# Placing the weight slots and the activation area at multiples of 1024 bytes in an fp32r transformer kernel

## What is computed

```python
x = x + 0.5 * swiglu(rmsnorm(x, ffn1_norm[l]), w_ffn1_in[l], w_ffn1_out[l])
u = rmsnorm(x, mix_norm[l])
c_q, c_kv, k_r, hq, hf, hi, hgate, mq, gate_logits = split_sizes(u @ w_in[l], IN_SPLITS)
y_mla = mla_branch(...) @ w_o_mla[l]        # causal attention from latents
y_hg = hgrn2_branch(...) @ w_o_hg[l]        # gated recurrence in chunks of 64
y_mem = memory_branch(...) @ w_o_mem[l]     # attention over 256 memory tokens
merged = gates[:, :, 0] * y_mla + gates[:, :, 1] * y_hg + gates[:, :, 2] * y_mem
x = x + merged @ w_out[l]
x = x + 0.5 * swiglu(rmsnorm(x, ffn2_norm[l]), w_ffn2_in[l], w_ffn2_out[l])
```

## The kernel before

| | address | mod 1024 | mod 64 |
|---|---|---|---|
| `x` (8192 bytes) | 16512 | 128 | 0 |
| `vecs`, gains and other small vectors (928 bytes) | 24704 | 128 | 0 |
| `c1`, constants | 25632 | 32 | 32 |
| `x_ssq`, `x_diag`, `x_sq` | 28736, 29760, 30784 | 64 | 0 |
| `raw0` to `raw2` | from 31904, every 8192 | 160 | 32 |
| `whi0` to `whi3` | from 56480, every 4096 | 160 | 32 |
| `wlo0` to `wlo3` | from 72864, every 4096 | 160 | 32 |
| `arena` | 90080 | 992 | 32 |

## Time and profile before

### The profile page before, as it was taken

How to read it: one execution, slowest core, us unless ns; L and a number is a source line. 1 busy time by engine, 2 the same in 40 slices (tenths; PEclk the granted TensorE clock), 3 DMA queues, 4 the chain that set the end, 5 groups by cost and what they waited for, 6 DMA issues and landing times.

```text
span 2501.2 us, 49272 instructions
## 1 busy us (share of the span) xinstructions
PE 2475.3 (99%) x20948; PEld 2416.1 (97%) x20948; DVE 1673.0 (67%) x2315; ACT 1279.4 (51%) x1812; POOL 406.9 (16%) x357
## 2 busy tenths in 40 slices
PE   9999999999999999999999999999999999999998
PEld 8999999999999999999999999999999999999998
DVE  7765776866667567877666666846666665846664
ACT  5544656554445455565444545535444444634543
POOL 4012120300200210102012014402011013512001
PEclk9999999999999999999999999999999999999999
DMA  6555433555555543345555554303555555402553
GB/s 238 186 186 186 159 128 122 191 192 189 179 190 188 179 176 139 120 164 186 186 186 211 191 197 167 117 18 134 187 186 185 186 186 182 152 2 86 196 185 126
DMA packets 57675, 410.11 MB, mean 164 GB/s; under 512 B 6384, under 2 KB 6640, under 8 KB 8688
## 3 DMA queue, kind: packets, MB, share of 16 engines
q1 hardware_dynamic: 56592, 402.15, 45.2%
q10 hardware_dynamic: 864, 4.82, 0.5%
HBM read 405.89 MB, written 1.05 MB: 163 GB/s over the span
## 4 chain that ended last, share of the span: by engine, by line
PE 88%; DVE 5%; issue 3%; ACT 3%; POOL 1%; DMA 0%; DVEq 0%; POOLq 0%; SPq 0%; ACTq 0%
PE bank L297 87%; DVE sb_wlo L310 2%; DVE area L310 2%; ACT area L306 1%; PE bank L301 1%; DVE area L321 1%; ACT sb_whi L306 1%; ACT L306 0%; POOL sb_x_ssq L310 0%; POOL sb_x_sq L310 0%; POOL area L310 0%; DVE sb_x L321 0%; DMA sb_raw<-stream 0%; DVE area L316 0%; DVE sb_x L310 0%
## 5 line engine op out<-in xcount | busy, mean ns | idle before, releaser
L297 PE MATMUL bank<-area,sb_whi 128*128 128x256 f32 x11752 | 2097.4, 281 | 9.1 <-DVE area L321 5.0
L297 PEld LDWEIGHTS bank<-area,sb_whi 128*128 128x128 f32 x11752 | 1803.7, 188 | 21.7 <-DVE area L321 8.2
L297 PE MATMUL bank<-area,sb_wlo 128*128 128x256 f32 x5876 | 1644.5, 280 | 4.5 <-DVE sb_wlo L310 4.3
L306 ACT ACTIVATE sb_whi<-sb_raw 128x1024 fp32r<-128x1024 f32 x762 | 801.9, 1058 | 780.4 <-PE bank L297 774.0
L297 PEld LDWEIGHTS bank<-area,sb_wlo 128*128 128x128 f32 x5876 | 1106.1, 188 | 6.3 <-DVE sb_wlo L310 6.3
L310 DVE TENSOR_TENSOR sb_wlo<-sb_raw,sb_whi 128x1024 fp32r<-128x1024 f32 x762 | 961.7, 1270 | 163.9 <-ACT sb_whi L306 162.7
L310 DVE TENSOR_TENSOR area<-area,area 128x256 f32<-128x256 f32 (+7 forms) x502 | 259.7, 526 | 249.9 <-ACT area L306 247.4
L306 ACT ACTIVATE area<-area 128x256 f32<-128x256 f32 (+6 forms) x515 | 252.1, 498 | 84.5 <-DVE area L310 60.1
L297 PE MATMUL bank<-area,area 128*64 128x64 f32 (+5 forms) x2304 | 211.7, 254 | 1.9 <-ACT area L306 1.9
L297 PEld LDWEIGHTS bank<-area,area 128*64 128x64 f32 (+2 forms) x2304 | 188.4, 157 | 20.5 <-ACT area L306 7.7
L310 DVE TENSOR_TENSOR area<-bank,sb_x_diag 128x512 f32<-128x512 f32 x244 | 167.0, 685 | 36.3 <-PE bank L297 21.9
(11 more groups left out here) (82 smaller groups left out, 706.1 us busy)
## 6 DMA issues: line engine op xcount, KB each, us to landing
sb_raw<-stream SPq DMA_DIRECT2D x379, 1024.0 KB, 4.8
sb_raw<-stream SPq DMA_DIRECT2D x4, 512.0 KB, 7.0
area<-lora ACTq DMA_DIRECT2D x2, 768.0 KB, 4.6
area<-c ACTq DMA_DIRECT2D x1, 1504.0 KB, 7.1
sb_x<-x SPq DMA_DIRECT2D x4, 256.0 KB, 5.2
area<-mem ACTq DMA_DIRECT2D x1, 1024.0 KB, 9.5
out<-sb_x SPq DMA_DIRECT2D x4, 256.0 KB, 2.9
area<-m ACTq DMA_DIRECT2D x1, 512.0 KB, 4.2
```

What stands on the lines that cost most here:

```text
L297: return lambda e: e.matmul(out, lhsT, rhs, start=start, stop=stop, skip_group_check=True, tile_position=at)
L306: return lambda e: e.activation(out, a, f, **kw)
```

## The change

Only addresses change. The raw, high and low weight slots are no longer allocated one by one but placed by hand below the area, and the area's start is rounded down to a multiple of 1024. The four slots are placed in two pairs, with 64 bytes left free below the slots of each pair. `vecs` moves behind the area. One allocation, `arena`, now covers all that is placed by hand. The instructions of every engine, their order, their shapes and their semaphores are the same in both programs.

```diff
+ROW = 1024
+LINE = 64
...
-    w.raw = [sbuf(k, f"raw{i}", [128, CHUNK_BLOCKS * 128]) for i in range(RAW_SLOTS)]
-    w.hi = [sbuf(k, f"whi{i}", [128, PIECE * 128], F32R) for i in range(SPLIT_SLOTS)]
-    w.lo = [sbuf(k, f"wlo{i}", [128, PIECE * 128], F32R) for i in range(SPLIT_SLOTS)]
+    at, piece = k.arena, 4 * PIECE * 128
+    w.hi, w.lo = [None] * SPLIT_SLOTS, [None] * SPLIT_SLOTS
+    for n in range(0, SPLIT_SLOTS, 2):
+        for name, group in (("whi", w.hi), ("wlo", w.lo)):
+            for i in (n, n + 1):
+                at -= piece
+                group[i] = k.nc.alloc_sbuf_tensor_at(f"sb_{name}{i}", [128, PIECE * 128], F32R, offset=at)
+        at -= LINE
+    w.raw = []
+    for i in range(RAW_SLOTS):
+        at -= 4 * CHUNK_BLOCKS * 128
+        w.raw.append(k.nc.alloc_sbuf_tensor_at(f"sb_raw{i}", [128, CHUNK_BLOCKS * 128], F32, offset=at))
+    assert at >= k.low, (at, k.low)
...
-        k.x, k.vecs, k.c1 = sbuf(k, "x", [128, NX, T]), sbuf(k, "vecs", [128, NV]), sbuf(k, "c1", [128, NC1])
+        k.x, k.c1 = sbuf(k, "x", [128, NX, T]), sbuf(k, "c1", [128, NC1])
         k.sx, k.scratch = scales(k, "x"), sbuf(k, "scratch", [128, 2])[:, :]
-        ctx.enter_context(nc.sbuf_tensor("arena", [128, ARENA], F32, side="right"))
-        k.arena, k.placed = nc.sbuf_usable_end // 32 * 32 - 4 * ARENA, 0
+        weights = 4 * 128 * (CHUNK_BLOCKS * RAW_SLOTS + 2 * PIECE * SPLIT_SLOTS)
+        end = nc.sbuf_usable_end // LINE * LINE
+        k.arena, k.placed = (end - 4 * ARENA - 4 * NV) // ROW * ROW, 0
+        k.low = k.arena - weights - 2 * LINE
+        ctx.enter_context(nc.sbuf_tensor("arena", [128, (nc.sbuf_usable_end - k.low) // 32 * 8], F32, side="right"))
+        k.vecs = nc.alloc_sbuf_tensor_at("sb_vecs", [128, NV], F32, offset=k.arena + 4 * ARENA)
```

## The result

The changed kernel took 2506.86 us (median of seven runs, 2504.96 to 2510.87) against 2500.7 us before: a ratio of 1.0025, 95% interval 1.0014 to 1.0036. That is a quarter of a per cent slower where 2.8% faster was forecast, and it is inside the range (2385 to 2508) only by its upper end. The quarter of a per cent itself should not be leaned on: in three later sessions the kernel before had medians of 2506.74, 2501.18 and 2501.6 us, and its single runs reach from 2498.9 to 2511.69. What has to be explained is that a forecast gain of 70 us did not come; that the time still lies inside the range is luck.

The account below looks back on a forecast made before the run. The prediction took the kernel to be bound by the spacing of PE's matmul starts. Narrow matmuls gain 70 us, all other terms 0: 2501.2 - 70 = 2431, so 2430 us against the 2500.7 median; range 2385 to 2508.

Parts of the forecast that it names:

- The stake: Excess of all 256-column (narrow) matmuls over pure streaming at 106.7 ns each: 187 us.
- the close spacing: Quicker of two paces seen for 256-column matmuls, 113.3 ns apart; forecast nearly throughout, chance 0.40, 2430 us.
- the term for the narrow matmuls: PE's 256-column matmuls: about 15,700 were to go from about 117.8 to 113.3 ns, gaining 70 us.
- one extra line: Reading of 6.7 ns over streaming as a straddled line; aligned operands would then reach 111.7 ns, 2402 us, chance 0.17.
- Rival (d): Slower: loads and moving reads meet more dearly, 122.2 ns; 2587 us for four slots, 2544 for two; chance 0.16.
- rival (b): Mixed: two distances alternate by slot, one at 113.3 ns and one at 117.8; half the gain, 2466 us; chance 0.17.
- Rival (c): Nothing: the instant of restart, not addresses, picks the matmul pace; time stays within 5 us; chance 0.10.
- The estimate by the same page's formula: Narrow matmul spacing as N / 2.4 + 2.5 ns: 109.2 ns, or 2359 us.
- wide matmuls: 312 matmuls of 512 columns, 20.0 ns above streaming each; between 0 and 6 us to gain, counted 0.
- Splits, loads and the rest of the chain: ACT and DVE weight splits and chunk loads, hidden beside matmuls, 0 us; other DVE and ACT chain work, plus or minus 4, taken 0.
- far kind: Slower of two paces seen for 256-column matmuls, about 117.8 ns apart, held by about 15,700 of them before.
- the load floor: Spacing of 128-column weight loads where only loads count, 111.7 ns each; taken as nearest floor for narrow matmuls.

Follow-up runs that it names:

- the fastest kernel: Changed kernel with every slot's high part 192 and low part 64 bytes below a multiple of 1024; 2449.02 us, ratio 0.9786 to the kernel before.
- off-by-32 kernel: Slots 64, 192, 320 and 448 bytes below a multiple of 1024, then area, weights, raw slots and small vectors all moved down 32 bytes; 2451.95 us, ratio 0.9802.
- all_at_0: Changed kernel with all four weight slots starting at a multiple of 1024, no 64 bytes left free; 2543.19 us, ratio 1.0143 to the kernel before.
- the mirror: Changed kernel with every slot's high part 64 and low part 192 bytes below a multiple of 1024; 2513.73 us.
- alternate_64_192: Changed kernel with slots 0 to 3 at 64, 192, 320 and 448 bytes below a multiple of 1024; 2453.49 us, ratio 0.9807 to the kernel before.
- alternate_0_64: Changed kernel with slots 0 to 3 at 0, 64, 256 and 320 bytes below a multiple of 1024; 2497.34 us.

## Why the prediction was wrong

The reading of the profile held. PE's spacing set the differences between the fourteen kernels; the clock, the other engines and DMA did not (the fastest kernel has 69% DVE share and the same mean granted clock, 0.994). That moving one of PE's two operands against the other changes the spacing was right (that it is their reads which meet is not shown, see below): fourteen placements of one program spread over 2449 to 2543 us with no instruction changed. The stake, 187 us, and the price of the close spacing, 70 us, were of the right size: the fastest kernel saved 68.3 us on narrow matmuls.

The step that failed is "I take the close spacing", in the term for the narrow matmuls: 15,700 x 4.45 = 70 us of gain, where their time went from 2033.9 to 2040.0 us. It rested on two grounds. One was that the close kind is the only other state the trace shows. But the trace of before shows a single distance modulo 256, and the new placement brings a second one beside it; at distance 0 there is a third state, 120.0 ns, which the earlier trace rows could not hold. The other ground was that lines not straddled and a distance of 0 or 512 speak for fewer meetings. The off-by-32 kernel shows that straddling counts for nothing (113.3 ns is its pace too, with all operands 32 bytes off a multiple of 64), so "one extra line" as a reading of the 6.7 ns falls, and `all_at_0` shows that 0 is the worst distance of those that are multiples of 64. For half of the matmuls I had the sign wrong: plus 2.6 ns where minus 4 was forecast. For the other half the spacing went down, by 2.2 ns on average, since only 62% of the pieces were close; and that half has the distance of before again (64 below, modulo 256), so that the change brought it no new distance at all.

Rival (d) had the place of the loss, distance 0 in two slots (the meeting of reads that it gives as the reason is not shown), and rival (b) the alternation; what came is the two at once. The rival's price was 122.2 ns against 120.0 measured, and its point of decision can be checked: with 120.0 in half the slots and 115.1 in the others the mean is 117.5, a shade above the present 117.3, and 17,600 x 0.2 is 3.5 us; the account has 6.1. The mistake lay in giving (b) and (d) as alternatives with the old spacings as their levels, not as one case with a loss in one half and a gain in the other, whose sum is near nothing.

Rival (c), nothing by address, falls by `all_at_0`. The Trainium skill, page "TensorE: Matmul & The Clock Gate", Step-by-step: what each phase is for, says that loading the next weights takes no read bandwidth from the running matmul. By it the distance of the two operands could change nothing, and between the best and the worst placement lie 3.8% of the time; so the runs speak against it for this case, without showing what it is that meets. The estimate by the same page's formula for the gap of a matmul by itself, 109.2 ns, was reached nowhere; the lowest steady pace in any kernel is 113.3.

The smaller terms: wide matmuls 0 counted, 0.8 us less measured, made of 226.7 ns in half of the slots and no gain in the others. Splits, loads and the rest of the chain 0 counted; "all else" moved by 0.2 us. The range reached the measured time by its upper end, but not for the reason given for that end, an unchanged spacing: that is luck.

## What stays open

Why the period is 256 bytes, why 64 below prefers the far kind and 192 below the close one, and why high 192 with low 64 is close while the mirror is not, no run here settles. Pieces entered by a step of the distance at a slot change are mostly close in three kernels (`alternate_64_192`, its copy off by 32, `alternate_0_64`); as a general rule this is refuted by the mirror and by the far stretches of the changed kernel. That the two things that meet are the weight load and the moving read is argued from their distance being all that matters; no kernel without weight loads was tried. Nor is it known what the last 6.7 ns over streaming are: the load floor of 111.7 ns is near, but not reached.

## What to carry to other kernels

When the spacing of back-to-back matmuls is above the column count over the clock and takes two values at one clock, count instructions per window and try the placement: shift the stationary operands against the moving ones by 64, 128 and 192 bytes and measure each, high and low parts apart. Try several in one program, one per buffer, and read them slot by slot; then confirm the uniform kernel, since what a slot does among its neighbours need not hold when all are alike. Round addresses are no aim in themselves: here equal remainders were the worst choice.

## What the runs showed of the hardware

- With fp32r operands of 128 x 128 and 128 x 256, full clock and no waits, the spacing depends on the distance of the two start addresses modulo 256 bytes: 120.0 ns at 0, 113.3 or 117.8 at 64 below, 118.3 at 128, 113.3 (less often 117.8) at 192. Displacing both by 32 bytes changes nothing (2453.49 and 2451.95 us); at distances of 32, 96, 160 and 224 no piece had 113.3 (means 116.6 to 119.9).
- The kind persists: over 1541 matmuls from 1345 to 1520 us in the kernel before, and in the changed kernel through pieces at distance 0 in between. In the kernel before, each of its seven changes between neighbouring pieces stands at a gap of 204 to 897 ns between two starts. Whether it also makes the times of one kernel differ (2498.9 to 2511.69 us over 34 runs of the kernel before) is not shown: in the seven runs of the changed kernel the three above 2509 us have a mean granted clock of 0.993 or 0.994, the four below 2507 us 0.995 to 0.997.
- Wide matmuls (moving 512 columns, weights moving and activations stationary) go the other way: 226.7 ns at distance 0, 233.3 in the placement before.
